# Scatter every block but the last to its own rows, put the last on its tokens with TensorE

## What is computed

```python
def moe_ffn(x, w_router, b_router, w_up, b_up, w_down, b_down):
    top_logit, top_idx = lax.top_k(x @ w_router + b_router, TOP_K)      # 4 of 32 experts
    gate = jax.nn.softmax(top_logit, axis=-1)
    ...                                       # sort (token, expert) pairs by expert, in blocks
    def block_fn(args):
        toks, g, e = args
        h_glu, h_lin = jnp.split(x[toks] @ w_up[e] + b_up[e], 2, axis=-1)
        ...                                   # clamps
        act = h_glu * jax.nn.sigmoid(SWIGLU_ALPHA * h_glu) * (h_lin + 1.0)
        return (act @ w_down[e] + b_down[e]) * g[:, None]
    return jax.ops.segment_sum(yb, tok_buf, num_segments=T)             # sum onto tokens
...
h = h + moe_ffn(rms_norm(h, norm2_gain), ...)
return rms_norm(h, final_gain)
```

## Time and profile before

| | us |
|---|---|
| device time, median of 3 runs | 1283.07 |
| lowest and highest | 1281.26, 1284.39 |
| the profiled execution, its own device time | 1284.14 |
| its span in the profile | 1282.4 |

### The profile page before, as it was taken

The page is one execution under the profiler, slowest core; times in us unless marked ns, Lnnn a source line. Parts: engine busy times, 40 slices in busy tenths (PEclk is TensorE's granted clock), DMA queues, the critical chain, the costliest instruction groups (busy, mean ns, idle before and its releaser), DMA issues.

```text
span 1282.4 us, 28381 instructions
## 1 busy us (share of the span) xinstructions
PE 1126.2 (88%) x11061; PEld 508.2 (40%) x11062; DVE 501.1 (39%) x1234; ACT 201.7 (16%) x293; POOL 223.7 (17%) x385
## 2 busy tenths in 40 slices
PE   9999999989799888899989798989898979797760
PEld 5445554544334433334434333434343434343220
DVE  1393454674333342333333233333233323332217
ACT  2104321122111111111111111111111111111101
POOL 1000112002212221212222121212121212121112
PEclk9999999999999998999999898989898989898875
DMA  9308307669999999999999999999999999999994
GB/s 344 133 33 290 104 5 301 278 260 394 423 429 383 427 428 429 431 428 429 427 427 431 431 426 431 428 429 426 430 431 428 428 429 429 427 431 427 429 377 164
DMA packets 55636, 469.21 MB, mean 366 GB/s; under 512 B 8616, under 2 KB 26396, under 8 KB 41136
## 3 DMA queue, kind: packets, MB, share of 16 engines
q1 hardware_dynamic: 45608, 447.29, 83.5%
q0 software_dynamic: 7776, 16.67, 3.5%
q10 hardware_dynamic: 2216, 4.75, 1.0%
HBM read 447.43 MB, written 25.04 MB: 368 GB/s over the span
## 4 chain that ended last, share of the span: by engine, by line
PE 55%; DMA 36%; DVE 4%; issue 2%; SPq 1%; POOL 0%; ACT 0%; POOLq 0%; DVEq 0%; ACTq 0%
DMA W<-in_w_up_dram 30%; PE B L1604 25%; PE B L1289 11%; PE B L1621 9%; PE B L1444 4%; DMA misc<-hsrow,idx_g 3%; PE B L1323 2%; DMA hres<-misc,idx_s 2%; DVE misc L1175 1%; DMA yrow<-misc,idx_s 1%; DVE W L1251 1%; SPq L323 1%; DMA W<-in_w_in_dram 0%; DVE W L1252 0%; DVE misc L1206 0%
## 5 line engine op out<-in xcount | busy, mean ns | idle before, releaser
L1604 PE MATMUL B<-W,misc 128*32 128x512 f32 x4992 | 585.2, 619 | 105.9 <-DMA W<-in_w_up_dram 80.8
L1604 PEld LDWEIGHTS B<-W,misc 128*32 128x32 f32 x4992 | 182.7, 114 | 462.1 <-issue 453.0
L1621 PE MATMUL B<-W,misc 128*32 128x256 f32 x4992 | 290.9, 384 | 11.5 <-DVE misc L1201 7.5
L1621 PEld LDWEIGHTS B<-W,misc 128*32 128x32 f32 x4992 | 182.9, 111 | 137.8 <-issue 61.6
L1175 DVE TENSOR_TENSOR misc<-B,misc 128x512 f32<-128x512 f32 x77 | 53.3, 692 | 310.6 <-PE B L1604 310.4
L713 ACT ACTIVATE misc<-misc 128x256 f32<-128x256 f32 x78 | 32.5, 417 | 819.2 <-DVE misc L1177 819.2
L1289 PE MATMUL B<-W 128*128 128x512 f32 x320 | 140.2, 593 | 0.0
L1192 DVE TENSOR_TENSOR misc<-B,misc 128x256 f32<-128x256 f32 x78 | 33.1, 425 | 190.6 <-POOL idx_s L535 163.7
L539 POOL DMA_INDIRECT yrow<-misc,idx_s x75 | 76.8, 1025 | 139.8 <-DVE misc L1194 139.8
L713 ACT ACT_TABLE_LOAD x78 | 100.1, 1283 | 5.7 <-DVE order_tab L1153 4.3
L526 POOL COPY idx_g<-idx_tab 128x1 uint32 (+1 forms) x77 | 14.1, 183 | 486.8 <-DVE misc L1206 477.8
(11 more groups left out here) (296 smaller groups left out, 521.7 us busy)
## 6 DMA issues: line engine op xcount, KB each, us to landing
W<-in_w_up_dram SPq DMA_DIRECT2D x56, 4096.0 KB, 32.9
W<-in_w_down_dram SPq DMA_DIRECT2D x28, 4096.0 KB, 30.5
W<-in_w_up_dram SPq DMA_DIRECT2D x16, 2048.0 KB, 15.0
W<-in_w_down_dram SPq DMA_DIRECT2D x8, 2048.0 KB, 18.2
W<-in_w_in_dram SPq DMA_DIRECT2D x5, 2048.0 KB, 16.5
yrow<-W SPq DMA_DIRECT2D x1, 8192.0 KB, 40.5
W<-yrow SPq DMA_DIRECT2D x4, 2048.0 KB, 29.1
W<-in_x_dram SPq DMA_DIRECT2D x8, 512.0 KB, 6.5
```

Of the source, the lines that this page charges most:

```text
L1604: ins = mm(B[0][BT * j:BT * (j + 1), :].rearrange("p (g n) -> p g n", g=2), xT[:, BT * k:BT * (k + 1)], up(par)[:, k, :, QC * j:QC * (j + 1)],
L1621: ins = mm(B[5][BT * j:BT * (j + 1), 0:QC], aT[:, BT * q:BT * (q + 1)], down(par)[:, q, QC * j:QC * (j + 1)], start=(q == 0), stop=(q == N ...
```

## The change

The accumulating scatters go. POOL's loop now scatters block 75 plainly too; block 76 (the one ahead of the last turn's first) has a row buffer `ylast` and an index column `idx_l` of its own, so that neither its `block_out` nor its scatter waits for the scatter ahead of it. If the last turn has more blocks, all but the last are scattered from `ysb` as ever. The last block is not scattered: its rows `yput` are multiplied on TensorE by `put`, a 0/1 matrix of rows by tokens that DVE makes from the block's token indices (`places_of`), in 16 products of 32 rows (`put_rows`). They are accumulated in PSUM on top of the residual, which TensorE puts there with the unit matrix (`add_tile`). `acc` names two banks for each of the four token tiles. The residual and the gain are loaded by ACT's queue as soon as block 76's down product is done; SP loads `yrow` once 77 scatters have landed, the last tile in three parts. DVE's finish is, for each tile, `sums` and then the PSUM banks added (`add_rest`). For the first two tiles ACT multiplies by the reciprocal root and POOL by the gain; DVE does both for the last two. The output is stored from `yfin`.

The core of the diff (declarations and the output loop are cut):

```diff
+        ylast, yput, put = tail(QC), tail(QC), tail(T)
+        acc = [(B[1], B[2]), (B[3], B[4]), (B[6], B[7]), (B[0], B[5])]
...
SP:
-            plain = sp.value_load(base_tab[0:1, NE - 2:NE - 1], ...)
+            written = sp.value_load(base_tab[0:1, NE + 1:NE + 2], ...)
             sp.wait_ge(m_u[3], done)
-            sp.wait_ge(m_sc, 16 * plain)
+            sp.wait_ge(m_sc, 16 * written)
-            for c in range(NT):
-                ... sp.dma_start(yfin[:, c, :], yrow[rows, :]...)
-            sp.wait_ge(m_y, done)
-            sp.dma_start(grow, final_gain...)
-            sp.wait_ge(f_ready, 1)
-            for c in range(NT):
-                ... sp.dma_start(hfin[:, c, :], hres[rows, :]...)
+            for c in range(NT - 1):
+                load_rows(c)
+            sp.dma_start(yfin[:, 3, 0:2 * D], places(3)[:, 0:2 * D]).then_inc(f_rows[3], 16)
+            sp.dma_start(yfin[:, 3, 2 * D:3 * D], places(3)[:, 2 * D:3 * D]).then_inc(f_rest, 16)
+            sp.dma_start(yfin[:, 3, 3 * D:4 * D], places(3)[:, 3 * D:4 * D]).then_inc(f_last, 16)
...
POOL, after the loop of gathers and plain scatters:
-            for back in (2, 1):
-                g = pool.value_load(base_tab[0:1, NE + back:NE + back + 1], ...)
-                pool.wait_ge(m_sc, 16 * g)
-                scatter_add(g)
-            pool.wait_ge(m_sc, 16 * total)
-            pool.memset(idx_s[:], 0).then_inc(f_ready, 1)
+            pool.wait_ge(m_y, written + 1)
+            pool.tensor_copy(idx_l, idx_y[:, bass.ts(written, 1)]).then_inc(m_is, 1)
+            pool.wait_ge(m_is, written + 1)
+            pool.wait_ge(m_ys, written + 1)
+            pool.indirect_dma_start(out=yrow, ..., in_=ylast, ...).then_inc(m_sc, 16)
+            pool.iota(tok_row_i, pattern=[[1, T]], base=0, channel_multiplier=0).then_inc(s_rc, 1)
...
             for c in range(NT):
                 rstd(st_f[:, c:c + 1], D, f_r)
+                if c < 2:
+                    pool.wait_ge(f_sq, 2 * c + 2)
+                    pool.tensor_tensor(yfin[:, c, 0:D], yfin[:, c, 0:D], grow, ALU.mult).then_inc(f_y, 1)
...
ACT, between the sigmoids of blocks 76 and 77:
+            act.wait_ge(m_y, done)
+            for c in range(NT):
+                act.dma_start(hfin[:, c, :], hres[rows, :]...).then_inc(s_tile[c], 16)
+            act.dma_start(grow, final_gain...).then_inc(s_late, 16)
...
DVE:
+            def places_of(g):
+                link(V.tensor_scalar(put_i, idx_tab[:, bass.ts(g, 1)], 2, None, ALU.logical_shift_right))
+                link(V.tensor_copy(put_f, put_i))
+                V.tensor_scalar(put, tok_row, put_f, None, ALU.is_equal).then_inc(f_put, 1)
...
                 if out_first:
-                    block_out(first, 1 - par)
+                    block_out(first, 1 - par, to=ylast)
+                    dve.wait_ge(s_rc, 8)
+                    link(V.tensor_copy(tok_row, tok_row_i))
+                    places_of(last - 1)
...
+            def add_rest(c):
+                dve.wait_ge(f_acc, ACC0 + c + 1)
+                for hf in range(2):
+                    ins = V.tensor_tensor(yfin[:, c, s], yfin[:, c, s], acc[c][hf][:], ALU.add)
...
+            block_out(total, 1, to=yput)
             for c in range(NT):
                 sums(c)
+                add_rest(c)
+            V.tensor_tensor(scaled, yfin[:, NT - 1, 0:D], grow, ALU.mult).then_inc(f_scaled, 1)
+            V.scalar_tensor_tensor(yfin[:, NT - 2, 0:D], ..., st_f[:, NT - 2:NT - 1], grow, ALU.mult, ALU.mult)
+            V.tensor_scalar(scaled, scaled, st_f[:, NT - 1:NT], None, ALU.mult)
...
PE:
+            def put_rows():
+                for early in (0, 1):
+                    for c in range(NT):
+                        for j in (early, early + 2):
+                            q = slice(BT * j, BT * (j + 1))
+                            ins = mm(acc[c][j // 2][:, ...], put[q, P * c:P * (c + 1)], yput[q, :],
+                                     start=False, stop=(early == 1))
...
                 block_up(first, par, lead, 16 * i + 16)
+                if out_first:
+                    for c in range(NT - 1):
+                        add_residual(c)
...
             block_down(total, 1, 16 * (NE // 2))
+            pe.wait_ge(m_ys, total)
+            pe.wait_ge(f_put, PUT0 + 1)
+            add_residual(NT - 1)
+            put_rows()
```

More of the change, by code:

```diff
@@ L559, in _ @@
             scatter(0)
-            with pool.Fori(4, add_from + 3) as g:
+            with pool.Fori(4, written + 3) as g:
                 pool.wait_ge(m_xT, g)
@@ L566, in _ @@
                 scatter(g - 3)
-            with pool.If_lt(pool.to_reg(add_from + 2), pool.to_reg(total)):
-                with pool.Fori(add_from + 3, total + 1) as g:
+            pool.wait_ge(m_y, written + 1)
+            pool.nop(nofuse=True)
+            pool.tensor_copy(idx_l, idx_y[:, bass.ts(written, 1)]).then_inc(m_is, 1)
+            pool.wait_ge(m_is, written + 1)
+            pool.wait_ge(m_ys, written + 1)
+            pool.nop(nofuse=True)
+            pool.indirect_dma_start(out=yrow, out_offset=bass.IndirectOffsetOnAxis(ap=idx_l, axis=0),
+                                    in_=ylast, in_offset=None, bounds_check=T * TOPK * H - 1, oob_is_err=False)\
+                .then_inc(m_sc, 16)
+            pool.iota(tok_row_i, pattern=[[1, T]], base=0, channel_multiplier=0).then_inc(s_rc, 1)
+            with pool.If_lt(pool.to_reg(written + 2), pool.to_reg(total)):
+                with pool.Fori(written + 3, total + 1) as g:
                     pool.wait_ge(m_xT, g)
@@ new lines, in sums @@
+                link(V.tensor_tensor(y[:, 0:D], y[:, 0:D], y[:, D:2 * D], ALU.add))
+                if c == NT - 1:
+                    dve.wait_ge(f_rest, 32)
+                    link(V.tensor_tensor(y[:, 0:D], y[:, 0:D], y[:, 2 * D:3 * D], ALU.add))
+            def add_rest(c):
+                dve.wait_ge(f_acc, ACC0 + c + 1)
+                for hf in range(2):
+                    s = slice(512 * hf, 512 * (hf + 1))
+                    ins = V.tensor_tensor(yfin[:, c, s], yfin[:, c, s], acc[c][hf][:], ALU.add)
+                if c < NT - 1:
+                    ins.then_inc(f_sum, 1)
+                else:
+                    link(ins)
+                    dve.wait_ge(f_last, 32)
+                    V.tensor_tensor(yfin[:, c, 0:D], yfin[:, c, 0:D], yfin[:, c, 3 * D:4 * D], ALU.add).then_inc(f_sum, 1)
@@ L1265, in _ @@
+            block_out(total, 1, to=yput)
             for c in range(NT):
                 sums(c)
[L1267 removed]
+                add_rest(c)
+            dve.wait_ge(f_sum, NT)
             dve.wait_ge(s_late, 16)
[L1269 to L1272 removed]
+            V.tensor_tensor(scaled, yfin[:, NT - 1, 0:D], grow, ALU.mult).then_inc(f_scaled, 1)
+            dve.wait_ge(f_r, NT - 1)
@@ L1624, in block_down, with add_tile, add_residual @@
                         ins.then_inc(m_yh if q == 3 else m_y, 1)
+            def put_rows():
[3 more added lines that the diff above has]
+                            q = slice(BT * j, BT * (j + 1))
+                            ins = mm(acc[c][j // 2][:, QC * (j % 2):QC * (j % 2 + 1)], put[q, P * c:P * (c + 1)],
+                                     yput[q, :], start=False, stop=(early == 1))
+                        if early:
+                            ins.then_inc(f_acc, 1)
+                    if not early:
+                        ins.then_inc(f_placed, 1)
+                        pe.wait_ge(f_placed, PLACED0 + 1)
+            def add_tile(c, rows):
+                for hf in range(2):
+                    ins = mm(acc[c][hf][:], ident[:], rows[:, 512 * hf:512 * (hf + 1)], start=True, stop=False)
+                return ins
+            def add_residual(c):
+                pe.wait_ge(s_tile[c], 32)
+                add_tile(c, hfin[:, c, :])
             def expert(par, i, first, last, out_first=False):
```

116 lines of the change are left out of this document (62 added, 54 removed).

## The result

| | before | changed |
|---|---|---|
| median, us | 1283.28 (12 runs) | 1287.07 (12 runs) |
| lowest to highest | 1281.02 to 1284.39 | 1284.68 to 1293.17 |
| the profiled execution, its span | 1284.14, 1282.4 | 1285.42, 1283.9 |

The ratio is 1.0041, 95% interval 1.0025 to 1.0058: 3.8 us by the medians, and slower where I had forecast 1278.2. The changed kernel's runs also lie 8.5 us apart, where those of before lie 3.4 apart.

The account below looks back on a forecast made before the run. Weights' DMA bounds the body, VectorE the finish behind block 76's down product (the point, 1227.66). First sum 1249.5 + 20.25 of sums + 0.8 for GpSimd + 7.0 gives 1277.55, 4.85 less: median 1278.2, range 1271 to 1284.

Parts of the forecast that it names:

- late engines: The few DMA engines whose backlog ends last, running back to back until 1257.7 before the change; transfers land when they finish.
- Block 76's rows: After block 76's down product: block_out done at 1228.7, scatter issued at 1229.5 and landed at 1239.3, bounds 1232.7 to 1244.5.
- The residual ahead of the last down product: Before block_down(78): waiting for weights and residual tiles, it starts at 1242.5, no better than before.
- The landing: Residual tiles behind the weights, 1.28 us each: the third at 1241.3, or 1243.9 with fourth tile and gain first.
- rival C: Slower: block 76's scatter releases all of yrow, so its first tile comes after 1254.4; at 22 us 1287.3; chance 0.07.
- The last down product: block_down(78), with TensorE idle ahead of it: 6.2 us as in the earlier trace, ending at 1248.7.
- The put products: TensorE, after the last block_out: first bank pair 3.7 us behind DVE, hidden by sums of 3.55; lower clock costs 3.
- rival D: Nothing gained: PSUM additions at the lower clock take back 3 us; median 1281.2; sign, DVE waiting for PE; chance 0.11.
- The lock: GpSimd's two gain multiplications in the finish holding DVE up: bounds 0 and 5.1 us, taken as 0.8.
- rival B: GpSimd locks DVE: the two multiplications cost the full 5.1 us; median 1282.5, no measurable change; chance 0.12.
- Arrival: During the sums: yrow tiles come every 5.1 us against 4.87 of work a tile, costing another 0.6.
- the tail: From the last sum to the end of the program: 7.0 us, against 6.8 before.

Follow-up runs that it names:

- y4: x4 with block 76's scatter left out (its rows missing from the output) and yrow loaded once block 75's scatter landed; ratio to the kernel before 0.9977.
- x3: Changed kernel with residual and gain loaded by SyncE's queue, between the last weights and yrow, instead of ScalarE's; ratio to the kernel before 1.0021.
- x4: Changed kernel with residual products behind the last down product, residual and gain on SyncE's queue, tiles 0 and 1's gain by VectorE; ratio to before 0.9987.
- y2: x4 with TensorE adding the fourth expert row for tiles 1 to 3, gain multiplications ahead of later PSUM additions; ratio to the kernel before 0.9967.
- y3: x4 with the residual added by VectorE instead of TensorE; ratio to the kernel before 1.0021.
- x1: Changed kernel with GpSimd's two multiplications by the final gain left out (tiles 0 and 1 stored without it); ratio to the kernel before 1.0017.
- x2: Changed kernel with TensorE's residual products of tiles 0 to 2 moved behind the last down product; ratio to the kernel before 1.0059.
- y1: x3 with the gain of tiles 0 and 1 multiplied by VectorE instead of ScalarE and GpSimd; ratio to the kernel before 1.0006.

## Why the prediction was wrong, step by step

All numbers behind the point; the forecast for the whole tail was 1277.55 - 1227.66 = 49.9, measured 58.9.

**What bounds the kernel before** stood as far as the runs show: the loss behind the point, +4.1 in the profiles, accounts for the +3.8 of the medians, and the late engines are real (y4).

**Block 76's rows** were right. The scatter was issued 1.8 us behind the point as forecast, and yrow was issued 8.8 later, close to the plain row of 9.84. **The token matrix** was right: 4.9 us behind the point, 2 us ahead of need.

**The residual ahead of the last down product is the step that failed:** start 21.9, against 14.8 forecast, +7.1. Two terms of it were wrong.

*The price of its products.* I had six products at 0.44, 2.6 us, which "fits" under the waits, and so put them at nothing. They took 6.58 + 1.98 = 8.56. I had read the 64 instructions of L1604 in a block as 64 products in 16 groups. The loops make 8 steps of 4, so `block_up` and `block_down` have 32 products in 8 groups each (the 64 products of the kernel's description are wrong too), and each product shows as two instructions: the two products of a residual tile as four, the 16 put products as 32. A product of 512 columns takes 2 x 0.49 = 0.98 at the higher clock. And behind 6.08 us of standing still TensorE ran at the lower one, where the eight instructions took 6.58. I had priced the down product at the lower clock, and these products in the same stretch at the higher. x3 tells what this term is worth: there the tiles landed at 11.5, 12.7 and 14.0, the third within my 13.6 to 16.2, and the down product still started at 19.0, 4.2 us later than the 14.8.

*The landing.* I had the third tile at 13.6 (and 16.2 with the fourth and the gain ahead of it) by adding bytes: late engines with 9.65 us of weights and 1.28 us a tile. It landed at 20.0. The two queues don't share by bytes. The first tile, 512 KB, landed with the 4 MB of weights (1237.9 and 1237.8), and when yrow was released the third and fourth paid a 2 MB tile's time each. I had put the yrow loads behind the residual in time, since they are issued 10 us later; in another queue they are not behind it. The bytes would have been right in one queue: x3's 1.3 us a tile. This term is the other 2.9 us, the difference between x3's start and the changed kernel's: 1.4 for the first tile, which landed at 12.9 instead of 11.5, 0.5 for the wait, and 1.0 because the products took 8.56 instead of 7.56. It is the smaller one, since the first two tiles kept TensorE busy until 19.5 anyway: of the third tile's delay only 0.49 was a wait.

No rival of mine had either. C had the right side, but by yrow's late release: in the changed kernel yrow's first tile landed at 1245.8, 5.7 us before the first sum began at 1251.54, and y4 shows that an earlier release doesn't bring it sooner.

**The last down product** took 3.66, not 6.2: the residual's products ran ahead of it, and the granted clock was 1.00, its 2.4 GHz level, from 1244 on. In x4, where it ran at 0.50 until about 1246, it took 6.50. That is -2.5: a part of the first error came back as a higher clock. First sum: 26.5, against 21.8.

**yrow** was nearly right: its first tile landed 20.7 behind the point, and 22.1 in x3 and x4, where I had 21.3 to 23.9.

**The put products** were not hidden: a wait of 1.67. Of it 1.06 is the fourth tile's residual, 1.96 where I had 0.9, and 0.15 stood in the forecast's own numbers, 3.7 of products under 3.55 of sums. The rest was not taken apart. It is rival D's sign, a wait for PE ahead of the first PSUM addition, but at the higher clock, where D asked for the lower. The 16 put products took 4.06, close to my 16 x 0.23 = 3.7, by luck: a product of 256 columns costs twice what I had (3.64/8 = 0.46 for a group), but these ran two at a time, 8 x 0.51. That they do is read from the time and from the order in `put_rows`; no run tests it.

**The lock** cost 4.06 where I took 0.8, between my bounds of 0 and 5.1, with no row behind the 0.8. I had let VectorE's unchanged times in the kernel before decide; there GpSimd's operations were one column wide, and what they take after VectorE's turn (0.4) fell in gaps. The PSUM additions cover nothing: GpSimd starts later, during the next two-input sum, and takes the following turn. This is rival B's mechanism at four fifths of its price. The Trainium skill (SBUF — State Buffer, "Who interferes with whom") says that a GpSimd instruction that reads SBUF and a VectorE one with two SBUF inputs hold each other up for a whole instruction; the trace agrees, with 2.03 us for each of two.

**Arrival** cost none of its 0.6, the sums themselves 0.3 less than 19.65, **the tail** 7.3 for 7.0. Together 4.7 + 1.7 + 3.3 - 0.6 - 0.3 + 0.3 = 9.1 of the 9.0 missed.

Smaller slips of the prediction: it takes 1249.5 for the first sum though it has VectorE busy until 1249.7; the down product's start at 1242.5 is 0.5 later than before, not earlier; and rival C adds 20.85 where the forecast's own terms give 20.25 + 0.8 = 21.05. None changes the verdict.

What was left of the gain? The waits on the accumulating scatters did go. The change as a whole is worth 2.7 us in the tail and 0.13% in x4, once three side effects are gone, and 0.33% in y2 when VectorE is relieved too. What the waits alone are worth, no run shows: y3 has none of them and is 1.0021, so the gain of x4 needs both the waits gone and the residual on TensorE, which spares VectorE four additions of 1.23 and so makes up for the additions from PSUM (4 x 1.28).

**Open.** The wide scatter of the changed kernel (8.5 us) is also there in x1 (10.2) and x2 (10.1), and narrower in x3 (4.5), y1 (4.8) and x4 (3.9). The three wide ones are those with two hardware queues; it may be the pairing of landings that varies, since x1's and the changed kernel's profiles differ by 3.2 us in the start of the down product, but two profiles don't show it. Which DMA engines run late, and why, was not examined.

## What to carry to other kernels

Before putting work of a few microseconds ahead of an operation on an in-order engine, price it at the clock that the engine will have there, and count instructions and products separately: the residual's products were thought to cost nothing, took 7.6 to 9.6 us behind idle time, and took back more than the scatter had cost. Before moving a small load to a second queue, look at what the first queue will hold when it is served: a small transfer can be made to pay the time of the large ones beside it. Work handed to GpSimd beside two-input VectorE operations is not free, and on the engine that bounds the stage it can be cheaper to do it there.

## What the runs showed of the hardware that I had not expected

- Two hardware DMA queues with work did not share the engines byte by byte; a small transfer took as long as a large one beside it: 512 KB tiles of ScalarE's queue landed at 1245.0, 1251.2 and 1257.3 beside 2 MB tiles of SyncE's at 1245.8, 1251.9 and 1258.0. A row of a tile is 4 KB in the one and 16 KB in the other, 128 rows each, so turns row by row would give this; the runs don't separate that from other ways. x1 and x2 show the same pattern, 6 us from tile to tile. In SyncE's queue, between weights and yrow, the same tiles were 1.3 us apart (x3).
- GpSimd's multiplication, waiting behind back-to-back two-input VectorE operations, got the turn at the next boundary, twice in each of the changed kernel, x2 and x3, and kept VectorE out for 2.03 us of a multiplication of 1024 columns; VectorE's operation is shown as running, 3.25 us long instead of 1.22, and not as idle.
- The down product of block 76 took 5.35 us in the changed kernel and 6.27 in the one before. Both stood behind idle time (4.33 and 4.05) and ran at a granted clock of 0.50 at first, which rose to 1.00 within 1222 to 1224 in the one and within 1226 to 1228 in the other. One behind unbroken work took 3.64. What sets the moment of the rise is not shown.
